# Two-block transformer kernel: gates, branch products and their sums kept transposed; sticks by sigmoids and a scan

## What is computed

```python
# first block (hybrid_mixer)
gates = jax.nn.sigmoid(h_gate).reshape(B, S, N_BRANCHES, D_MODEL)
merged = (gates[:, :, 0] * jnp.einsum('bsk,kd->bsd', a, w_br_mla)
          + gates[:, :, 1] * jnp.einsum('bsk,kd->bsd', b, w_br_moba)
          + gates[:, :, 2] * jnp.einsum('bsk,kd->bsd', c, w_br_dil))
return jnp.einsum('bsd,de->bse', merged, w_out)
# second block (_hybrid_mixer)
proj = jnp.einsum('bsrc,rcd->bsrd', branches, w_branch)
gates = jax.nn.sigmoid(gpre.reshape(b, s, N_BRANCH, D_MODEL) + gate_bias)
return jnp.einsum('bsrd,bsrd->bsd', gates, proj) @ w_out
# third branch of the second block (_stick_breaking)
log_stay = jnp.where(strict, jax.nn.log_sigmoid(-z), 0.0)
after = lax.cumsum(log_stay, axis=3, reverse=True) - log_stay
a = jnp.where(strict, jnp.exp(jax.nn.log_sigmoid(z) + after), 0.0)
```

## Time and profile before

| | us |
|---|---|
| median of three runs | 2859.56 |
| the profiled execution | 2859.51 |
| its span, first to last instruction | 2857.7 |
| TensorE busy | 2825.0 (99%) |
| TensorE's weight loads busy | 2502.9 (88%) |
| VectorE busy | 1832.8 (64%) |
| ScalarE busy | 1486.6 (52%) |
| GpSimd busy | 230.8 (8%) |
| DMA engines, mean busy share | 49.0% in the main queue |
| mean granted TensorE clock | 0.999 |

### The profile page before, as it was taken

The page is one execution under the profiler, slowest core; times in us unless marked ns, Lnnn a source line. Parts: engine busy times, 40 slices in busy tenths (PEclk is TensorE's granted clock), DMA queues, the critical chain, the costliest instruction groups (busy, mean ns, idle before and its releaser), DMA issues.

```text
span 2857.7 us, 44578 instructions
## 1 busy us (share of the span) xinstructions
PE 2825.0 (99%) x18116; PEld 2502.9 (88%) x18116; DVE 1832.8 (64%) x2727; ACT 1486.6 (52%) x2308; POOL 230.8 (8%) x187
## 2 busy tenths in 40 slices
PE   9999999999999999999999999999999999999998
PEld 8989879989989779989888887899899888878997
DVE  6656675646656666645468778765554687786655
ACT  5445555444445645444456567444444465675442
POOL 0010001010010011010014000010100131000100
PEclk9999999999999999999999999999999999999999
DMA  6544435545544445555554344555555554444553
GB/s 238 192 165 158 157 142 179 191 177 192 192 165 153 148 155 198 190 194 185 192 190 177 133 160 154 206 196 179 195 189 192 181 183 147 156 151 181 206 199 119
DMA packets 74779, 504.09 MB, mean 176 GB/s; under 512 B 8752, under 2 KB 10448, under 8 KB 18768
## 3 DMA queue, kind: packets, MB, share of 16 engines
q1 hardware_dynamic: 74576, 501.24, 49.0%
HBM read 500.12 MB, written 1.08 MB: 175 GB/s over the span
## 4 chain that ended last, share of the span: by engine, by line
PE 84%; DVE 8%; ACT 4%; POOL 2%; issue 1%; DMA 0%; SPq 0%; DVEq 0%; ACTq 0%
PE ps L1524 41%; PE ps L1542 37%; PE ps L1563 2%; DVE wlo L1996 2%; POOL wlo L2452 1%; DVE conv L2290 1%; DVE pr L2392 1%; ACT whi L1728 1%; DVE sm L2393 1%; ACT pr L1957 1%; PE ps L1658 1%; DVE pr L2389 1%; ACT pr L1963 1%; ACT pr L1955 1%; POOL stat L2429 1%
## 5 line engine op out<-in xcount | busy, mean ns | idle before, releaser
L1728 ACT ACTIVATE whi<-raw 128x1024 fp32r<-128x1024 f32 (+3 forms) x938 | 976.5, 1043 | 867.4 <-PE ps L1524 436.0
L1996 DVE TENSOR_TENSOR wlo<-raw,whi 128x1024 fp32r<-128x1024 f32 (+2 forms) x894 | 1080.2, 1220 | 303.2 <-ACT whi L1728 301.7
L1542 PE MATMUL ps<-xT_hi,whi 128*128 128x256 f32 x3296 | 927.0, 281 | 2.1 <-DVE wlo L1996 1.1
L1542 PE MATMUL ps<-xT_lo,whi 128*128 128x256 f32 x3296 | 920.4, 279 | 0.0
L1542 PE MATMUL ps<-xT_hi,wlo 128*128 128x256 f32 x3296 | 919.9, 279 | 0.0
L1542 PEld LDWEIGHTS ps<-xT_hi,whi 128*128 128x128 f32 x3296 | 619.4, 188 | 9.5 <-issue 6.9
L1542 PEld LDWEIGHTS ps<-xT_lo,whi 128*128 128x128 f32 x3296 | 619.6, 188 | 0.5
L1542 PEld LDWEIGHTS ps<-xT_hi,wlo 128*128 128x128 f32 x3296 | 619.4, 188 | 0.0
L1524 PE MATMUL ps<-whi,xT_hi 128*128 128x512 f32 (+2 forms) x1152 | 368.4, 401 | 1.7 <-ACT whi L1728 0.9
L1524 PE MATMUL ps<-wlo,xT_hi 128*128 128x512 f32 (+2 forms) x1152 | 355.4, 389 | 0.1
L1524 PE MATMUL ps<-whi,xT_lo 128*128 128x512 f32 (+2 forms) x1152 | 355.2, 389 | 0.0
(11 more groups left out here) (318 smaller groups left out, 2418.0 us busy)
## 6 DMA issues: line engine op xcount, KB each, us to landing
raw<-in_w SPq DMA_DIRECT2D x436, 1024.0 KB, 4.8
vr<-in_vrows SPq DMA_DIRECT2D x19, 512.0 KB, 5.7
raw<-in_w SPq DMA_DIRECT2D x12, 768.0 KB, 4.2
raw<-in_w SPq DMA_DIRECT2D x10, 896.0 KB, 4.6
...
```

What stands on the lines that cost most here:

```text
L1542: made = e.matmul(out, ws[:, o:o + 128], xs[:, kt, :], start=kt == 0 and n == 0 and c % 2 == 0, stop=kt == job.nk - 1 and n == 2, skip_gro ...
L1728: e.activation(out, raw, ACT.Copy).then_inc(*mark("hi", i))
L1996: e.tensor_tensor(out, raw, hi.bitcast(F32), sub).then_inc(*mark("lo", i))
```

## The change

The gates and the branch products of both mixers are made with `gemm_w`, so gates, products and sums have channels on partitions; ScalarE and VectorE write the sum's high and low part to xT straight away (`halve_o` in the fiber `merged`), with no transpose. All sums are added by VectorE. During the last branch, `slack` makes `take` queue low halves only up to u+1. In the first block the dilated branch is second, its output transposed in the fiber `second` into tiles 6 and 7 of xT, and `heads` no longer skips pieces. In the second block the gate bias is a per-partition column, so ScalarE makes the gates from PSUM in one operation a tile; the bias rows' DMAs and GpSimd's additions are gone. A stick head takes sigmoid(-z) and sigmoid(z), a reverse scan that multiplies and takes the maximum with a table that is one at the ends, and a product; `keep` becomes `ends`.

```diff
-BR1 = [(0, "w_br_mla", 3), (1, "w_br_moba", 3), (2, "w_br_dil", 2)]
+BR1 = [(0, "w_br_mla", 3), (2, "w_br_dil", 2), (1, "w_br_moba", 3)]
...
-        for part, upto in ((0, self.u + self.reach), (1, self.u + NHL - 1)):
+        for part, upto in ((0, self.u + self.reach), (1, self.u + NHL - 1 - self.slack)):
...
-                if s % 3 == 2:
-                    yield
...
-            toks = self.gemm(("g1", l, c), xt, 8, [[(b, 0, 512)] for b in banks], free)
-            for t in (0, 1):
-                self.do("gate1", l, c, t, banks[t], toks[t])
-                gate[c, t] = ("gate", "g1", l, c, t)
-                self.main.put(banks[t], gate[c, t])
+            tok = self.gemm_w(("g1", l, c), xt, 8, slices(banks), free)
+            for k, b in zip((4 * c, 4 * c + 2), banks):
+                self.do("gate1", l, k, b, tok)
+                gate[k] = ("gate", "g1", l, k)
+                self.main.put(b, gate[k])
         self.drain()
-        xt.free = (toks[1],)
-        third = lambda: self.to_T([m["o_dil"][:, t, :] for t in (0, 1)], (("vec", "dil_o", l),), 2, oTa)
-        self.branches("br1", l, [(r, nk) for r, _, nk in BR1], [oTa, oTb, oTa], m["g1"], gate,
-                      [m["xn"][:, t, :] for t in (0, 1)], self.xn_free, iter(()), third, 1.0)
+        xt.free = (tok,)
+        oTd = Halves("oTd", xt.H[:, 6:8, :], xt.L[:, 6:8, :], 2)
+        oTd.gen, oTd.free = l, xt.free
+        def second():
+            yield
+            self.to_T([m["o_dil"][:, t, :] for t in (0, 1)], (("vec", "dil_o", l),), 2, oTd)
+        self.branches("br1", l, [(r, nk) for r, _, nk in BR1], [oTa, oTd, oTb], m["g1"], gate,
+                      tiles_of(m["xn"]), self.xn_free, second(), None, 1.0)
         self.product_out("o1", l, then, 0.5)
...
     def branches(self, key, l, order, ots, G, gate, dst, dst_free, second, third, plus):
         xt = self.m["xT"]
         self.fibers.append(second)
+        def merged(n):
+            for k in (4 * n, 4 * n + 2):
+                there = (xt.name, xt.gen, k)
+                self.do("halve_o", there, dst[:, k:k + 2, :], ("vec", "merged", key, l, k), xt, k, 2, xt.free)
+                xt.ready[k] = xt.ready[k + 1] = [("xlo", *there)] * 2
+            self.xn_free = (("xlo", *there),)
+            xt.gen += n
+            yield
         for i, (r, nk) in enumerate(order):
+            last = i == len(order) - 1
+            self.slack = 2 if last else 0
             for n in (0, 1):
                 banks, free = self.two()
-                def merge(t, tok):
-                    a = dst[t][:, 512 * n:512 * n + 512]
-                    g = G[:, t, 1024 * r + 512 * n:1024 * r + 512 * n + 512]
-                    self.do("merge", key, l, i, n, t, a, g, banks[t], tok, gate[2 * r + n, t], plus, dst_free)
-                    self.main.put(banks[t], ("merge", key, l, i, n, t))
-                late = i == len(order) - 1 and n == 1
-                def mid(tok):
-                    merge(0, tok)
-                    for t in (0, 1):
-                        self.xn_free = (self.turn(dst[t], (("vec", "merged", key, l, 0, t),), t, 0, xt),)
-                toks = self.gemm((key, l, r, n), ots[i], nk, [[(b, 0, 512)] for b in banks], free,
-                                 mid if late else None)
-                if not late:
-                    merge(0, toks[0])
-                merge(1, toks[1])
-            ots[i].free = (toks[1],)
+                tok = self.gemm_w((key, l, r, n), ots[i], nk, slices(banks), free)
+                for k, b in zip((4 * n, 4 * n + 2), banks):
+                    self.do("merge", key, l, i, k, flat(dst[:, k:k + 2, :]), flat(G[:, 8 * r + k:8 * r + k + 2, :]), b,
+                            tok, gate[8 * r + k], plus, dst_free)
+                    self.main.put(b, ("merge", key, l, i, k))
+                if last:
+                    self.fibers.append(merged(n))
+            ots[i].free = xt.free = (tok,)
             if i == 0:
-                third()
                 assert second not in self.fibers
-        def other_half():
-            for t in (0, 1):
-                self.xn_free = (self.turn(dst[t], (("vec", "merged", key, l, 1, t),), t, 4, xt),)
-            xt.gen += 1
-            yield
-        self.fibers.append(other_half())
+                if third:
+                    third()
+        self.slack = 0
...
-                    pT[h] = self.turn_probs(("c", l, h), w_of[h], ("exp", "c", l, h), prs, pts)
+                    pT[h] = self.turn_probs(("c", l, h), z_of[h], ("vec", "stick", l, h), prs, pts)
-                    sms.put(z_of[h], ("exp", "c", l, h))
+                    sms.put(w_of[h], ("vec", "stick", l, h))
-                    z, z_free = sms.get()
-                    w, w_free = prs.get()
+                    z, z_free = prs.get()
+                    w, w_free = sms.get()
...
-            if c % 2 == 0:
-                row, i, there = self.vrow((l, f"gb{c // 2}"))
-            toks = self.gemm(("g2", l, c), xt, 8, [[(b, 0, 512)] for b in banks], free)
-            for t in (0, 1):
-                self.do("gate2", l, c, t, G[:, t, 512 * c:512 * c + 512], banks[t],
-                        row[:, 512 * (c % 2):512 * (c % 2) + 512], toks[t], there, fence3)
-                self.main.put(banks[t], ("merge", "gate2", l, c, t))
-            if c % 2:
-                self.vr_free[i] = (("merge", "gate2", l, c, 0), ("merge", "gate2", l, c, 1))
+            tok = self.gemm_w(("g2", l, c), xt, 8, slices(banks), free)
+            for k, b in zip((4 * c, 4 * c + 2), banks):
+                self.do("gate2", l, k, G, b, tok, fence3)
+                gate[k] = ("gate", "g2", l, k)
+                self.main.put(b, gate[k])
             if c == 3:
                 self.to_T([ob[:, t, :] for t in (0, 1)], fence2[0:2], 8, oT, self.col("ssm_norm_g_2", l, 8))
-        xt.free = (toks[1],)
-        def sigmoid(r, t):
-            self.do("sigmoid", l, r, t, G[:, t, 1024 * r:1024 * r + 1024])
-            gate[2 * r, t] = gate[2 * r + 1, t] = ("gate", "sig", l, r, t)
-        def gates():
-            while rest in self.fibers:
-                yield
-            for r in (0, 2):
-                for t in (0, 1):
-                    sigmoid(r, t)
-                    yield
-        for t in (0, 1):
-            sigmoid(1, t)
-        self.do("log_table")
-        self.fibers.append(gates())
+        xt.free = (tok,)
...
+    def gate2(l, k, G, bank, tok, fence):
+        b = COLS[("gate_bias_2", l)] + k
+        act.wait_ge(*at(*tok))
+        act.wait_ge(*at(*fence[0]))
+        for j in (0, 1):
+            made = e.activation(G[:, k + j, :], bank[:, 256 * j:256 * j + 256], ACT.Sigmoid,
+                                bias=m["cols"][:, b + j:b + j + 1])
+        made.then_inc(*mark("gate", "g2", l, k))
...
     def stick_scores(l, h, ps, z, z_free, w, w_free):
         for f in w_free:
-        e.activation(w[:, :], z[:, :], ACT.Abs).then_inc(*mark("act", "abs", l, h))
-        act.wait_ge(*at("act", "abs", l, h))
-        e.activation(w[:, :], w[:, :], ACT.Exp, scale=-1.0).then_inc(*mark("act", "abs_e", l, h))
-        act.wait_ge(*at("act", "abs_e", l, h))
-        e.activation(w[:, :], w[:, :], ACT.Ln, bias=1.0).then_inc(*mark("act", "soft", l, h))
-    def stick(l, h, z, w):
-        act.wait_ge(*at("vec", "stick", l, h))
-        e.activation(w[:, :], z[:, :], ACT.Exp).then_inc(*mark("exp", "c", l, h))
-    def sigmoid(l, r, t, g):
-        act.wait_ge(*at("merge", "gate2", l, 2 * r, t))
-        act.wait_ge(*at("merge", "gate2", l, 2 * r + 1, t))
-        e.activation(g, g, ACT.Sigmoid).then_inc(*mark("gate", "sig", l, r, t))
+        e.activation(w[:, 0:384], z[:, :], ACT.Sigmoid, scale=-1.0).then_inc(*mark("act", "leaves", l, h))
+        act.wait_ge(*at("act", "leaves", l, h))
+        e.activation(z[:, :], z[:, :], ACT.Sigmoid).then_inc(*mark("act", "takes", l, h))
...
-    def merge(key, l, i, n, t, a, g, bank, tok, gate, plus, free):
+    def merge(key, l, i, k, a, g, bank, tok, gate, plus, free):
         dve.wait_ge(*at(*tok))
         dve.wait_ge(*at(*gate))
         if i == 0:
             for f in free:
                 dve.wait_ge(*at(*f))
-            e.scalar_tensor_tensor(out=a, in0=g, scalar=plus, in1=bank[:, :], op0=add, op1=mul
-                                   ).then_inc(*mark("merge", key, l, i, n, t))
-        else:
-            e.scalar_tensor_tensor(out=g, in0=g, scalar=plus, in1=bank[:, :], op0=add, op1=mul
-                                   ).then_inc(*mark("merge", key, l, i, n, t))
-        if i == 2:
-            dve.wait_ge(*at("merge", key, l, i, n, t))
-            dve.wait_ge(*at("merge_p", key, l, n, t))
-            e.tensor_tensor(a, a, g, add).then_inc(*mark("vec", "merged", key, l, n, t))
+        e.scalar_tensor_tensor(out=g if i else a, in0=g, scalar=plus, in1=bank[:, :], op0=add, op1=mul
+                               ).then_inc(*mark("merge", key, l, i, k))
+        if i:
```

(35 more changed lines are left out.)

49 lines of the change are left out of this document (24 added, 25 removed).

## The result

The changed kernel takes 2863.91 us (median of 22 runs, 2863.11 to 2864.98) against 2859.38 for the kernel before (22 runs): a ratio of 1.0016, 95% interval 1.0010 to 1.0022. That is 4.5 us slower, inside 0.2%, and 10.1 us above the 2853.8 that I forecast; it is also outside the range. The profiled execution took 2863.9 us with a span of 2861.9.

The account below looks back on a forecast made before the run. TensorE, busy 99% of the span, was taken as the bound. Terms: 3.8 us net from transposed gates and products, less 2.0 for heads, plus 3.8 from sticks, 5.7 us unrounded, so 2853.8 us; range 2850 to 2858.

Parts of the forecast that it names:

- The bound: Whole kernel: TensorE busy 99% of the span, so only work off its queue or its waits move the time.
- 0.456 ns a column in both forms: Distance between matmul starts on TensorE: 116.7 ns for 256 columns, 233.3 for 512, taken as the same pitch.
- by the pitch they cost TensorE nothing: Gates and branches: 82 pieces a pair of mixers change from rows to columns at no cost to TensorE.
- Removed at the branches' ends, 16.0 us: Ends of branches, four mixers: transposes and waits removed, 6.05 + 6.56 + 2 x 1.7 = 16.0 us.
- new waits, 12.2: Last branch and output product: TensorE waits on late low halves and xT_lo, 3.0 or 3.1 us a layer, 12.2 in all.
- Rival B: Late low halves don't hold TensorE up, as VectorE is ahead; 12.2 us come back, 2841.6; chance 0.18, whole or half.
- goes with the pause: First block, layer 1, end of branches: the clock's dip, 0.5 us against layer 0, vanishes with the pause.
- Moba heads, 1.0 us a layer: First block's heads without spare slot: two more steps wait for VectorE's norm, 1.0 us a layer, 2.0 in all.
- Rival D: First block's heads run in lockstep with VectorE without spare slots, 21.6 us on top, 2875; chance 0.07.
- Sticks, 1.9 us a layer: Second block's stick heads: waits for pt (0.77 us) and behind ob's turns (1.1) go, 3.8 us in all.
- Rival C: Gates on ScalarE and the turns of ob leave the sticks' waits as they were, 2857.6; chance 0.15.
- Rival E: Fixed 2.5 ns per matmul, 12 more in each of 164 pieces, 2858.7; sign: pitch over 117 ns; chance 0.02.

Follow-up runs that it names:

- a_shift_back: Changed kernel with unused bytes so every tile stands at the same distance from a 128-byte boundary as in the kernel before; 2857.87 us, ratio 0.9995.
- a_slack0: Changed kernel with `self.slack = 0` in the last branch instead of 2; 2856.57 us, ratio 0.9989.
- a_x176h216: Changed kernel with slack 0, xT placed 176 and hT 216 bytes behind a 256-byte boundary by unused bytes; 2812.47 us, ratio 0.9836.
- a_x176entry: a_x176h216 with one small product more ahead of the first block's four feed-forwards, no address changed; 2798.24 us, one run.
- a_best3: The same program as a_x176entry, timed against the kernel before; 2798.65 us, ratio 0.9788.
- a_entry: Changed kernel with slack 0, xT 16 and hT 216 behind a 256-byte boundary, one small product more ahead of the first block's feed-forwards; 2838.97 us, one run.
- b_sticks: Kernel before with the new stick heads alone, gates and branches still rows, addresses kept to the 128-byte remainder; 2855.13 us, ratio 0.9986.
- b_shift: Kernel before with only unused bytes added, so every tile stands at its address in the changed kernel; 2861.81 us, ratio 1.0007.

## Why the prediction was wrong, point by point

**The bound.** Right: TensorE at 99%, and waits on its queue are what an edit moves. But "0.456 ns a column in both forms" was read from one stage and carried to all. This is the step that failed. Of the 10.1 us, 6.0 came from it through the shifted addresses. The same step stands in "by the pitch they cost TensorE nothing", said of the 82 pieces that change from rows to columns, and it failed a second time in a_shift_back: columns on the second block's oT run 117.8 ns there, where half a rows product on it took 116.7 and 116.2 in its two branches before, some 0.5 us a layer over 384 products. oT stands 384 bytes further on in a_shift_back, so its place may have a part in this.

**Removed at the branches' ends, 16.0 us, and new waits, 12.2.** In the first block a_shift_back is shorter by 1.8 and 2.4 us (table) where these terms and the heads say 2.05 and 2.6: right. The new waits came at the three places and with nearly the worked sizes: 0.81, 0.78 and 0.99 us for 0.8, 1.1 and 1.1; 1.37, 0.4 and 1.0 for 1.5, 0.5 and 1.1. Rival B is refuted. The clock's dip went with the pause, in the changed kernel and in a_slack0; other kernels with the change have a dip at the first block's branches all the same (a_x176h216, a_x176entry, a_best3 and a_entry, granted clock 0.57 to 0.72 over four microseconds). So "goes with the pause" held for this program and is no rule.

**What I didn't see in them.** That VectorE was idle for 6.38 us ahead of these merges. The order `slack = 2` was a choice and not a need, and undoing it was worth 7.3 us; my expectation for a_slack0 repeated the belief that VectorE was full there.

**Moba heads, 1.0 us a layer.** Two more waits of 0.46 and 0.30 us by the rows, 1.1 by starts: right, and the spare slots would have cost more at o_dil. Rival D, a lockstep of all heads, is refuted: no other head waits.

**Sticks, 1.9 us a layer.** The 0.77 us on pt went. Behind the turns 0.5 of 1.6 us went and not 1.1: oT_hi starts 2.64 us behind the turns (1743.13 - 1740.49) where it was 3.12 (1743.82 - 1740.70 by the earlier trace rows), 0.5 us earlier and not 1.2. This term was mis-sized by 0.6 us a layer, in the direction of its lower bound; b_sticks shows that the gates' evictions are what eats it. Rival C holds for that half of the term alone.

**The rest of the miss.** 6.0 us for the shift, 1.2 for the sticks and up to 1.0 for columns on oT make some 8.2 of 10.1. About 2 us stay without a name. By the table of a_shift_back 0.8 of them lie in the second block's mixers, which lose 0.9 and 1.1 us there where my terms had them gain 0.5 each, and 0.4 in the first block's. The rest lies outside the mixers; the start of the first feed-forward alone varies from 35.3 to 37.0 us among the traces.

**Rival E and its sign.** I wrote that a distance over 117 ns in 256-column products would prove a fixed cost per matmul. It came, 118.3 ns, and proved nothing: b_shift shows it with not one product more. Where both forms are in their fastest rhythm, columns take 113.4 and rows 226.7 ns, 0.443 ns a column in both. The Trainium skill (TensorE: Matmul & The Clock Gate, section Back-to-back issue gap) has 2.5 ns on top of the columns in its formula for the gap of an isolated matmul, and says that a stream of them doesn't keep to it; I had applied it to a stream. These two figures leave no room for such a part. The count was off as well: the changed kernel has 1,856 matmuls more, which are 1,920 for 80 whole pieces a pair of mixers less 64 transposes, since four of my 82 hold half a piece.

**The range.** It took in waits of every size and no change of the distance. One row more of the trace of before, the second feed-forward, would have shown a spread of 1% in the distance; 1% of TensorE's 2825 us is 28.
